# Two key tiles of the memory attention move from the tail into the latent attention

## The chip, the cores and the metric

The kernel runs on one core of a Trainium2 chip. The metric is the time on the device in microseconds (us), the median of several executions; lower is better.

## The reference

Two transformer blocks of different kind run one after the other, each two layers deep, on 512 tokens of width 1024 (float32). The change lies in the second block. Of one of its layers this matters here:

```
y_a, y_b, y_c = three mixers of other kinds          # 256 columns each
y_d = mla(...)          # "latent attention": 4 heads of 96, 512 x 512 scores
cat = rms_norm of [y_a, y_b, y_c, y_d], in four groups of 256 columns
x = x + cat @ w_out
hq = rms_norm(x, g_xq);  mn = rms_norm(mem, g_mem)   # mem: 256 rows of 1024
q = hq @ x_wq;  k, v = split(mn @ x_wkv)             # "memory attention"
o = attention(rms_norm(q), rms_norm(k), v);  x = x + o @ x_wo
x = x + (silu(a1) * a3) @ f_w2
```

The keys k of the memory attention need only the memory and the weights, nothing of x.

## The kernel before

**Weights.** Every weight matrix comes in tiles of 128 x 1024, which pass one stream (class `Weights`). SP loads a tile (L352) into one of two `raw` buffers (`RING`) as soon as the low part of the tile two places before it is made. ScalarE (ACT) makes its high part (L361, `split_high`), GpSimd (POOL) its low part (L370, `split_low`), into three buffers each (`PARTS`). TensorE (PE) multiplies a tile by activations that are split in the same way: three matmuls for each 128 rows (L384 to L386, `product`), 24 for a tile. The order of the tiles is fixed; the two key tiles have the numbers `base` and `base + 1`, the eight of w_out follow, then query and value tiles.

**Stages.** A stage is a block in which each engine has its own list of instructions; semaphores join them, and all engines meet at a barrier (L331) at its end. In a layer of the second block the mixers are followed by `second_attention` (the latent attention) and `second_tail` (norm of cat, w_out, memory attention, feed-forward part).

**The latent attention.** `attention_work` writes 16 units (4 heads by 4 blocks of 128 queries), n = 0 to 15. For each, PE multiplies the scores (L737), VectorE (DVE) takes the maximum (L835) and its negative (L838), ACT the exponentials (L799), DVE the reciprocal of their sum (L848, in the next step), POOL the scaled probabilities (L874), PE transposes them ("turn", L745), ACT copies the transposed block (L808), and after eight units PE multiplies by the values (L751, "values"). A turn comes four steps after its scores. PE goes in steps of two units: scores of n and n + 1, turns of n - 4 and n - 3, and at steps 12 and 20 the values. Each engine has side work between its steps. On DVE and ACT that is the preparation of the memory (`memory_prep`, class `Prep`): in steps 3 to 10 DVE makes high parts (L517), low parts (L527) and sums of squares (L534) of the eight chunks of the memory, in steps 2 to 9 ACT the squares (L523). ACT splits a weight tile in steps 10, 12 and 14, POOL behind units 12 and 14. POOL multiplies branch b (L2350) behind units 8 and 10. After its last copy (unit 15) ACT loads a table, does two SiLU, loads a table again and squares four tiles (L2319 to L2324), then copies the last values out (L817).

**The tail's start.** PE sums squares over the partitions for the four groups of cat (`group_sum`, L2424, four instructions each), and between them does the total of the memory (L539, L2434) and the two key tiles:

```
group_sum(0); group_sum(1); memory.total(...); columns
key_tile(0)
group_sum(2)
group_sum(3)
key_tile(1)
pe.wait_ge(sem("cat_log"), 4)
```

ACT makes Ln and Exp of each group's sum (L2525, L2527), then splits the tile `base + 3`, then makes the high parts of chunks 0 to 3 of cat (L2520). DVE multiplies the norm in (L2619) and makes the low parts (L2624). The first w_out matmul on PE waits for the low part of chunk 0, and each further chunk k of the first two w_out tiles for its own low part. The square of the keys (L2537), their sum over a head and the finished keys (L2650) come while PE is at the w_out tiles. The change and the prediction touch these places.

Of the kernel before, what the change touches and what calls it, by code (L numbers as in the profile page):

```python
# [18 lines left out]
ALU = mybir.AluOpType  # L19
ACT = mybir.ActivationFunctionType  # L20
# [3 lines left out]
P = 128  # L24
SEQ = 512
NT = SEQ // P
D = 1024
# [4 lines left out]
EPS = 1e-6  # L32
MEM = 256
# [552 lines left out]
def build(nc, x_in, w1, small1, const_in, p_in, w2, small2, masks_in, mem_in, pos_in, out):  # L586
    sem = Semaphores(nc)
# [9 lines left out]
    S = sb("slots", [P, SLOTS, SEQ])  # L597
# [7 lines left out]
    tmp = sb("tmp", [P, 10, SEQ])  # L605
# [17 lines left out]
    def cst(name):  # L623
        a, b = CONST.at[name]
        return const[:, a:b]
# [5 lines left out]
    def s2(name, i=0, n=1):  # L631
        a, _ = SECOND_SMALL.at[name]
        return small[:, a + i:a + i + n]
# [1664 lines left out]
    def second_attention(layer, weights, memory):  # L2298

        base = weights.used  # L2300

        def before(sp):
            sp.dma_start(S[:, MEM_RAW:MEM_RAW + 4, :].rearrange("p a (b n) -> p (a b) n", b=2), mem_in).then_inc(sem("load_mem"), 16)

        def first_act(act):
            for slot in (DEVIATION, B_R, B_R + 1):
                act.activation(S[:, slot, :], S[:, slot, :], ACT.Exp, scale=-0.5).then_inc(sem("late_rstd"), 1)

        def side_act(act, step):
            if step == 2:  # L2310
                act.wait_ge(sem("load_mem"), 16)
            if 2 <= step < 2 + KC:
                memory.square(act, step - 2)
            if step in (10, 12, 14):
                weights.split_high(act, base + step // 2 - 4)
            if step == 4 * NT + 3:
                for c in range(2):
                    act.wait_ge(sem("standard"), c + 1)
                    act.activation(S[:, Y + c, :], S[:, TAP_A + c, :], ACT.Silu, scale=s2("ln_g", c), bias=s2("ln_b", c)).then_inc(sem("branch_a"), 1)  # L2319
                act.preload_act_table_set(LOG_EXP)  # L2320
                act.wait_ge(sem("branch_a"), 2)
                act.wait_ge(sem("branch_b"), 2)
                for n in range(4):
                    act.activation(tmp[:, n, :], S[:, Y + n, :], ACT.Square).then_inc(sem("early_square"), 1)  # L2324

        def side_dve(dve, step, place):
            if place == "end" and step in (3, 4):
                a = S[:, TAP_A + step - 3, :]
                if step == 3:
                    dve.wait_ge(sem("late_rstd"), 3)  # L2330
                dve.tensor_tensor(a, a, S[:, DEVIATION, :], ALU.mult).then_inc(sem("standard"), 1)
            if place == "end" and step in (5, 6):
                c = step - 5
                y = S[:, Y + 2 + c, :]
                dve.scalar_tensor_tensor(y, y, s2("onorm", c), S[:, B_R + c, :], ALU.mult, ALU.mult).then_inc(sem("b_normed"), 1)
            if place == "scores" and step == 3:
                dve.wait_ge(sem("load_mem"), 16)
            if place == "scores" and 3 <= step < 3 + KC:
                memory.high_dve(dve, step - 3)
                if step >= 4:  # L2340
                    memory.add(dve, step - 3)
            if place == "end" and 3 <= step < 3 + KC:
                memory.low(dve, step - 3)

        def side_pool(pool, n):
            if n in (8, 10):
                c = (n - 8) // 2
                y = S[:, Y + 2 + c, :]
                pool.wait_ge(sem("b_normed"), c + 1)
                pool.tensor_tensor(y, y, S[:, G + c, :], ALU.mult).then_inc(sem("branch_b"), 1)  # L2350
            if n in (12, 14):
                weights.split_low(pool, base + n // 2 - 5)

        attention(weights, base + 3, attention_work(one(
            4, 1, 96 ** -0.5, lambda h, m, i: S[0:96, MQ + h, i * P:i * P + P], lambda h, m, L: S[0:96, MK + h, 0:L],
            lambda i: SEQ, None, lambda h, j: S[:, MV + j // 2, (j % 2) * 256 + 64 * h:(j % 2) * 256 + 64 * h + 64], 64,
            lambda h: S[64 * (h % 2):64 * (h % 2) + 64, Y + 6 + h // 2, :], NT, False,
            query_col=lambda h, i: col[:, QUERY_R + 4 * h + i:QUERY_R + 4 * h + i + 1]),
            side_act=side_act, side_dve=side_dve, side_pool=side_pool), before, first_act)

    def second_tail(layer, weights, memory, lead):

        base = weights.used
        out_at = base + 2
        q_at = out_at + KC
        o_at = q_at + 4
# [41 lines left out]
        with nc.Block() as block:  # L2408
# [10 lines left out]
            def _(pe):  # L2419
                def group_sum(g):  # L2420
                    if g >= 2:
                        pe.wait_ge(sem("cat_square"), 2 * g - 2)
                    for c in range(2):
                        mm = pe.matmul(banks[7 - g][:, :], cst("ones"), tmp[:, 2 * g + c, :], start=(c == 0), stop=(c == 1))  # L2424
                    mm.then_inc(sem("cat_summed"), 1)

                def key_tile(c):
                    dense(pe, weights, banks[2][:, c * MEM:c * MEM + MEM], memory.pairs)

                group_sum(0)  # L2430
                group_sum(1)
                memory.total(pe, banks[3][:, 0:MEM], cst("ones"), carried=True)
                for i in range(2):
                    mm = pe.matmul(banks[3][:, MEM + i:MEM + i + 1], memory.acc[:, i * P:i * P + P], cst("ones")[:, 0:1], start=True, stop=True)  # L2434
                mm.then_inc(sem("mem_columns"), 1)
                key_tile(0)
                group_sum(2)
                group_sum(3)
                key_tile(1)
                pe.wait_ge(sem("cat_log"), 4)  # L2440
                two = []
                for g in range(4):
# [36 lines left out]
                    mm.then_inc(sem("tile_done"), 1)  # L2479

                pe.wait_ge(sem("x_mixed"), KC)
                value_half(0)
                for c in range(2):
                    pe.wait_ge(sem("query_square"), c + 1)
# [29 lines left out]
            def _(act):  # L2514
# [7 lines left out]
                for g in range(4):  # L2522
                    act.wait_ge(sem("cat_summed"), g + 1)
                    r = tmp[:, 2 * g + 1, :]
                    act.activation(r, banks[7 - g][:, :], ACT.Ln, scale=1.0 / 256, bias=eps).then_inc(sem("cat_log"), 1)  # L2525
                    act.wait_ge(sem("cat_log"), g + 1)
                    act.activation(r, r, ACT.Exp, scale=-0.5).then_inc(sem("cat_rstd"), 1)  # L2527
                    if g == 1:
                        act.wait_ge(sem("mem_columns"), 1)
                        act.activation(col[:, MEM_R:MEM_R + 2], banks[3][:, MEM:MEM + 2], ACT.Ln, scale=1.0 / D, bias=eps).then_inc(sem("mem_column"), 1)  # L2530
                        act.wait_ge(sem("mem_column"), 1)
                        act.activation(col[:, MEM_R:MEM_R + 2], col[:, MEM_R:MEM_R + 2], ACT.Exp, scale=-0.5).then_inc(sem("mem_rstd"), 1)
                weights.split_high(act, base + 4)
                for n in range(4):
                    cat_high(n)
                act.wait_ge(sem("tile_done"), base + 2)
                act.activation(K_SQ, banks[2][:, :], ACT.Square).then_inc(sem("key_square"), 1)  # L2537
                weights.split_high(act, base + 5)
                for n in range(4, KC):
                    cat_high(n)  # L2540
# [73 lines left out]
            def _(dve):  # L2614
# [16 lines left out]
                normed(3)  # L2631
                dve.wait_ge(sem("mem_total"), 1)
                dve.wait_ge(sem("mem_columns"), 1)
                dve.tensor_scalar(E64_MEM, banks[3][:, 0:MEM], 64 * EPS / D, 64 * EPS * EPS, ALU.mult, ALU.add).then_inc(sem("mem_eps"), 1)
                cat_low(2)
                cat_low(3)
                for c in range(KC):
                    dve.wait_ge(sem("tile_done"), out_at + c + 1)
                    dve.tensor_tensor(S[:, X + c, :], S[:, X + c, :], banks[4 + c % 2][:, :], ALU.add).then_inc(sem("x_mixed"), 1)
                    hq.low(dve, c)  # L2640
                    if c >= 1:
                        hq.add(dve, c)
                    if c == 3:
                        dve.wait_ge(sem("key_sum"), 1)
                        dve.wait_ge(sem("mem_eps"), 1)
                        dve.tensor_tensor(K_R.rearrange("p (a n) -> p a n", a=2), banks[3][:, :].rearrange("p (a n) -> p a n", a=2),
                                          E64_MEM.unsqueeze(1).to_broadcast([P, 2, MEM]), ALU.add).then_inc(sem("key_biased"), 1)
                    if c == 5:
                        dve.wait_ge(sem("key_rstd"), 1)
                        dve.scalar_tensor_tensor(S[:, XK, :], banks[2][:, :], s2("x_kn"), K_R, ALU.mult, ALU.mult).then_inc(sem("key_ready"), 1)  # L2650
                dve.wait_ge(hq.sig("total"), 1)
                dve.tensor_scalar(E64, banks[6][:, :], 64 * EPS / D, 64 * EPS * EPS, ALU.mult, ALU.add).then_inc(sem("query_eps"), 1)
                dve.wait_ge(sem("query_eps"), 1)
# [94 lines left out]
```

## Time and profile before

| what | us |
|---|---|
| median of 3 executions | 3237.43 (3234.82 to 3238.01) |
| the profiled execution, its own time | 3235.97 |
| span of the profiled execution, first to last instruction | 3234.2 |
| latent attention, first of the two layers, from the trace | 1911.7 to 1961.7 |
| start of its tail, up to the first w_out matmul | 1961.7 to 1978.1 |
| latent attention, second layer | 2692.5 to 2743.2 |
| start of its tail, up to the first w_out matmul | 2743.2 to 2759.6 |

The mean granted clock of TensorE over the span is 0.987 of the full 2.4 GHz. Times in the trace count from the start of the span. In a row of a timeline, what stands in brackets is how long the engine sat idle before the instruction, and who ended that; PEq is the sequencer of TensorE, "issue" is a wait that the profile can't name. PE is the matmul, PEld the loading of its weights. "xN" joins N instructions in a row.

### The profile page before, as it was taken

How to read it: one execution, taken by the hardware profiler on the slowest of the kernel's cores; microseconds unless marked ns; L12 is line 12 of the kernel's file. 1: busy time of each engine (PE TensorE's matmuls, PEld its weight loads, DVE VectorE, ACT ScalarE, POOL GpSimd, SP SyncE). 2: the span in 40 equal slices, each digit the busy share in tenths (PEclk: the TensorE clock that was granted, in tenths of full speed). 3: DMA queues.
4: the chain of work that ended last, by engine and by line, in shares of the span. 5: the costliest groups of instructions: out<-in, count | busy, mean ns of one | idle time of the engine just before them, and what ended most of it. 6: DMA issues, size and time to landing. Idle time of an engine off the chain costs nothing. (4 is left out here: it accounts for less than half of the span.)

```text
span 3234.2 us, 38506 instructions
## 1 busy us (share of the span) xinstructions
PE 3076.4 (95%) x14372; PEld 2395.9 (74%) x14372; DVE 1624.8 (50%) x2472; ACT 1343.9 (42%) x2218; POOL 1589.8 (49%) x870
## 2 busy tenths in 40 slices
PE   8989999999999999999999988899999987989999
PEld 6766788888766678888887746688888763768887
DVE  3873357732477435774348754433224954443321
ACT  4446533333443654333342475532233267452221
POOL 5635655554663455555565343344445534344443
PEclk9999999999999999999999999999999998999999
DMA  4211233233221123333322102133332201223333
GB/s 134 66 59 46 85 101 96 97 111 98 89 70 60 46 75 102 98 98 108 106 97 79 47 14 65 59 104 92 98 109 93 72 27 33 72 72 98 98 98 104
DMA packets 73737, 265.05 MB, mean 82 GB/s; under 512 B 8656, under 2 KB 9168, under 8 KB 73168
## 3 DMA queue, kind: packets, MB, share of 16 engines
q1 hardware_dynamic: 73552, 262.59, 25.7%
q8 instruction: 115, 1.88, 0.2%
q14 instruction: 70, 0.57, 0.1%
HBM read 260.46 MB, written 2.10 MB: 81 GB/s over the span
## 5 line engine op out<-in xcount | busy, mean ns | idle before, releaser
L370 POOL TENSOR_TENSOR low<-raw,high 128x1024 fp32r<-128x1024 f32 x482 | 1178.7, 2447 | 1157.0 <-ACT high L361 1120.8
L385 PE MATMUL bank<-slot_r,low 128*128 128x512 f32 (+1 forms) x3652 | 1427.5, 391 | 0.0
L386 PE MATMUL bank<-slot_r,high 128*128 128x512 f32 (+1 forms) x3652 | 1425.4, 390 | 0.0
L384 PE MATMUL bank<-slot_r,high 128*128 128x512 f32 (+1 forms) x3332 | 1326.3, 398 | 45.4 <-POOL low L370 14.9
L361 ACT ACTIVATE high<-raw 128x1024 fp32r<-128x1024 f32 x482 | 508.2, 1056 | 908.4 <-PE bank L386 838.5
L386 PEld LDWEIGHTS bank<-slot_r,high 128*128 128x128 f32 x3652 | 689.2, 189 | 148.3
L385 PEld LDWEIGHTS bank<-slot_r,low 128*128 128x128 f32 x3652 | 689.5, 189 | 146.0 <-issue 6.7
L384 PEld LDWEIGHTS bank<-slot_r,high 128*128 128x128 f32 x3332 | 629.4, 189 | 216.8 <-issue 50.3
L1618 DVE SCALAR_TENSOR_TENSOR tmp<-padded,small,tmp 128x512 f32<-128x512 f32 x176 | 210.0, 1252 | 0.0
L874 POOL TENSOR_SCALAR tmp<-tmp,stat 128x512 f32<-128x512 f32 (+3 forms) x128 | 80.3, 628 | 148.3 <-DVE stat L848 123.0
L2107 DVE SCALAR_TENSOR_TENSOR slots<-padded,small,slots 128x512 f32<-128x512 f32 x128 | 140.4, 1154 | 0.0
L1609 DVE TENSOR_TENSOR padded<-bank,rs 128x512 f32<-128x512 f32 x88 | 60.4, 687 | 138.6 <-PE bank L386 128.9
L2677 DVE TENSOR_TENSOR tmp<-bank,rs 128x512 f32<-128x512 f32 x44 | 30.4, 692 | 191.9 <-PE bank L386 186.7
L737 PE MATMUL bank<-slots 64*128 64x256 f32 (+4 forms) x384 | 97.3, 509 | 22.2 <-PEq L331 19.3
L527 DVE SCALAR_TENSOR_TENSOR slot_r<-slots,small,slot_r 128x512 fp32r<-128x512 f32 (+1 forms) x80 | 92.8, 1160 | 44.1 <-ACT slot_r L514 43.8
L808 ACT ACTIVATE PT<-bank 128x256 f32<-128x256 f32 (+3 forms) x160 | 72.0, 454 | 102.4 <-PE bank L751 58.6
L2589 ACT ACTIVATE tmp<-tmp 128x512 f32<-128x512 f32 x44 | 28.0, 636 | 203.1 <-DVE tmp L2677 203.1
L2687 DVE TENSOR_TENSOR tmp<-bank,rs 128x512 f32<-128x512 f32 x16 | 11.1, 691 | 193.9 <-PE bank L386 193.9
L745 PE MATMUL bank<-const,tmp 128*128 128x128 f32 x432 | 72.7, 291 | 36.7 <-ACT PT L808 27.9
L1361 DVE TENSOR_TENSOR slot_r<-tmp,slot_r 128x512 fp32r<-128x512 f32 x48 | 75.6, 1575 | 59.4 <-ACT slot_r L2582 59.4
L745 PEld LDWEIGHTS bank<-const,tmp 128*128 128x128 f32 x432 | 51.7, 146 | 67.8 <-issue 38.9
L384 PE MATMUL bank<-pt_r,high 128*128 128x512 f32 x256 | 101.6, 397 | 0.0
(310 smaller groups left out, 3165.8 us busy)
## 6 DMA issues: line engine op xcount, KB each, us to landing
raw<-w SPq DMA_DIRECT2D x482, 512.0 KB, 3.6
slots<-x_in SPq DMA_DIRECT2D x4, 512.0 KB, 6.6
slots<-mem_in SPq DMA_DIRECT2D x2, 1024.0 KB, 4.8
out<-slots SPq DMA_DIRECT2D x8, 256.0 KB, 5.1
const<-const_in SPq DMA_DIRECT2D x1, 1073.5 KB, 10.7
padded<-p_in SPq DMA_DIRECT2D x2, 512.0 KB, 5.6
tmp<-masks_in SPq DMA_DIRECT2D x1, 512.0 KB, 11.5
small<-small SPq DMA_DIRECT2D x2, 231.5 KB, 2.9
```

Of the source, the lines that this page charges most:

```text
L361: act.activation(self.high[:, t % PARTS, :], self.raw[:, t % RING, :], ACT.Copy).then_inc(self.sem("tile_high"), 1)
L370: pool.tensor_tensor(self.low[:, t % PARTS, :], self.raw[:, t % RING, :], self.high[:, t % PARTS, :].bitcast(F32), ALU.subtract).then_inc( ...
L384: pe.matmul(acc, lhs[0], rhs[1], start=first, stop=False)
L385: pe.matmul(acc, lhs[1], rhs[0], start=False, stop=False)
L386: return pe.matmul(acc, lhs[0], rhs[0], start=False, stop=last)
L527: dve.scalar_tensor_tensor(self.pairs[c][1], self.xs[c], self.gain[c], self.pairs[c][0].bitcast(F32), ALU.mult, ALU.subtract).then_inc(sel ...
L737: pe.matmul(banks[s % 4][:, 0:width(n)], a["q"](h, m, i), a["k"](h, m, width(n)), start=True, stop=True).then_inc(sem("scored"), 1)
L745: mm = pe.transpose(banks[4 + n % 2][:, j * P:j * P + P], prob(n)[:, j * P:j * P + P], cst("ident"))
L874: pool.tensor_scalar(prob(n), tmp[:, E + s % 4, 0:width(n)], st(3, s), 1.0, ALU.mult, ALU.mult).then_inc(sem("prob_ready"), 1)
L1361: dve.tensor_tensor(parts[g][1], tmp[:, 6 + g % 2, :], parts[g][0].bitcast(F32), ALU.subtract).then_inc(sem("hidden_low"), 1)
L1618: dve.scalar_tensor_tensor(o, padded_t[:, s % 4, 15 - tap:15 - tap + SEQ], s1("conv_w", (2 - tap) * 2 * FC + ch), o, ALU.mult, ALU.add).th ...
L2107: ins = dve.scalar_tensor_tensor(o, src, s2(w, 2 * j + c), o, ALU.mult, ALU.add)
```

## The change

The two key tiles are multiplied in the latent attention, in PE's steps 14 and 16, behind the turns (turns 10 and 11, and 12 and 13), into bank 7, which that attention does not use. So that the tiles are there, ACT splits in steps 6, 8 and 14 instead of 10, 12 and 14, and POOL behind units 7 and 9 instead of 12 and 14; the third tile's low part is made at the start of the tail, as before. In the tail the key tiles fall away, the group sums and the memory's total use other banks (6 to 3, and 2), and one wait for the finished keys stands ahead of the value tiles, which write bank 7. No instruction is added or dropped but waits.

```diff
@@ second_attention
-            if step in (10, 12, 14):
-                weights.split_high(act, base + step // 2 - 4)
+            if step in (6, 8, 14):
+                weights.split_high(act, base + {6: 1, 8: 2, 14: 3}[step])
...
-            if n in (12, 14):
-                weights.split_low(pool, base + n // 2 - 5)
+            if n in (7, 9):
+                weights.split_low(pool, base + (n - 5) // 2)
+
+        def side_pe(pe, step, place):
+            if place == "turns" and step in (14, 16):
+                c = (step - 14) // 2
+                dense(pe, weights, banks[7][:, c * MEM:c * MEM + MEM], memory.pairs, norm=memory)
...
@@ second_tail
-        base = weights.used
+        base = weights.used - 2
...
-                        mm = pe.matmul(banks[7 - g][:, :], cst("ones"), tmp[:, 2 * g + c, :], start=(c == 0), stop=(c == 1))
+                        mm = pe.matmul(banks[6 - g][:, :], cst("ones"), tmp[:, 2 * g + c, :], start=(c == 0), stop=(c == 1))
...
-                def key_tile(c):
-                    dense(pe, weights, banks[2][:, c * MEM:c * MEM + MEM], memory.pairs)
...
-                memory.total(pe, banks[3][:, 0:MEM], cst("ones"), carried=True)
+                memory.total(pe, banks[2][:, 0:MEM], cst("ones"), carried=True)
...
-                key_tile(0)
                 group_sum(2)
                 group_sum(3)
-                key_tile(1)
                 pe.wait_ge(sem("cat_log"), 4)
...
                 pe.wait_ge(sem("x_mixed"), KC)
+                pe.wait_ge(sem("key_ready"), 1)
                 value_half(0)
...
-                act.wait_ge(sem("tile_done"), base + 2)
-                act.activation(K_SQ, banks[2][:, :], ACT.Square).then_inc(sem("key_square"), 1)
+                act.activation(K_SQ, banks[7][:, :], ACT.Square).then_inc(sem("key_square"), 1)
...
-                        dve.scalar_tensor_tensor(S[:, XK, :], banks[2][:, :], s2("x_kn"), K_R, ALU.mult, ALU.mult).then_inc(sem("key_ready"), 1)
+                        dve.scalar_tensor_tensor(S[:, XK, :], banks[7][:, :], s2("x_kn"), K_R, ALU.mult, ALU.mult).then_inc(sem("key_ready"), 1)
```

## Rows read from the trace of the kernel before

**Rows 1.** The page: busy time of each engine.

```profile
PE 3076.4 (95%) x14372; PEld 2395.9 (74%) x14372; DVE 1624.8 (50%) x2472; ACT 1343.9 (42%) x2218; POOL 1589.8 (49%) x870
```

**Rows 2.** Stages: PE, PEld, DVE, ACT, POOL busy, clock, DMA, GB/s.

```profile
1911.70:1961.70 50.00, 36.35 (x128) 17.36 (x128) 25.81 (x75) 37.08 (x74) 21.60 (x20) 0.86 0.10 32
...
1978.00:1992.00 14.00, 13.93 (x48) 11.01 (x48) 9.87 (x13) 3.04 (x5) 2.83 (x1) 0.78 0.27 75
...
2759.50:2772.90 13.40, 12.77 (x48) 9.86 (x48) 10.03 (x13) 3.04 (x6) 2.83 (x1) 0.89 0.24 78
```

**Rows 3.** Chain that ended last, second tail: start, us, what.

```profile
2750.70 3.45 PE bank L2424 x8
...
2754.17 0.70 ACT tmp L2525
...
2755.43 1.05 ACT high L361
...
2757.03 1.61 DVE slot_r L2624
```

**Rows 4.** Timeline of PE, first tail: start, us, idle before.

```profile
1961.78 3.67 PE L2424 MATMUL bank<-tmp,const 128*128 128x512 f32 x8 [3.04 <-PEq L331]
...
1966.08 0.37 PE L384 MATMUL bank<-slot_r,high 128*128 128x256 f32 x1
...
1969.05 3.60 PE L2424 MATMUL bank<-tmp,const 128*128 128x512 f32 x8
...
1972.08 0.68 PE L384 MATMUL bank<-slot_r,high 128*128 128x256 f32 x1
...
1978.07 0.77 PE L384 MATMUL bank<-slot_r,high 128*128 128x512 f32 x1 [2.57 <-issue]
```

**Rows 5.** Timelines of ACT, DVE and POOL where DVE and POOL overlap.

```profile
1931.81 0.78 ACT L799 ACTIVATE tmp<-bank,stat,col 128x512 f32<-128x512 f32 x1 [0.24 <-DVE stat L838]
...
1931.69 0.34 DVE L517 TENSOR_SCALAR slot_r<-slots,small 128x256 fp32r<-128x256 f32 x1
...
1933.59 1.18 DVE L517 TENSOR_SCALAR slot_r<-slots,small 128x256 fp32r<-128x256 f32 x1
...
1937.43 0.67 DVE L835 TENSOR_REDUCE stat<-bank 128x1 f32<-128x512 f32 x1
...
1975.54 2.43 DVE L2624 TENSOR_TENSOR slot_r<-tmp,slot_r 128x512 fp32r<-128x512 f32 x1 [7.25 <-ACT slot_r L2520]
...
1930.63 0.85 POOL L874 TENSOR_SCALAR tmp<-tmp,stat 128x512 f32<-128x512 f32 x1 [1.05 <-DVE stat L848]
...
1933.35 1.27 POOL L2350 TENSOR_TENSOR slots<-slots 128x512 f32<-128x512 f32 x1
...
1937.23 1.27 POOL L2350 TENSOR_TENSOR slots<-slots 128x512 f32<-128x512 f32 x1
...
1975.07 2.36 POOL L370 TENSOR_TENSOR low<-raw,high 128x1024 fp32r<-128x1024 f32 x1 [10.88 <-ACT high L361]
```

**Rows 6.** Timelines of PE and ACT, end of the first latent attention.

```profile
1945.67 0.63 PE L745 MATMUL bank<-const,tmp 128*128 128x128 f32 x4 [1.16 <-ACT PT L808]
...
1949.87 2.78 PE L745 MATMUL bank<-const,tmp 128*128 128x128 f32 x12 [1.57 <-ACT PT L808]
...
1953.34 5.40 PE L751 MATMUL bank<-PT,slots 128*64 128x512 f32 x16 [0.69 <-ACT PT L808]
...
1942.26 0.60 ACT L808 ACTIVATE PT<-bank 128x512 f32<-128x512 f32 x1 [3.70 <-PE bank L751]
...
1943.23 1.05 ACT L361 ACTIVATE high<-raw 128x1024 fp32r<-128x1024 f32 x1
...
1952.68 0.60 ACT L808 ACTIVATE PT<-bank 128x512 f32<-128x512 f32 x1 [0.42 <-PE bank L745]
```

**Rows 7.** Stages: PE, PEld, DVE, ACT, POOL busy, clock, DMA, GB/s.

```profile
1911.70:1919.60 7.90, 7.82 (x21) 3.83 (x22) 5.08 (x15) 5.65 (x13) 2.38 (x3) 0.78 0.39 133
...
2692.50:2700.30 7.80, 7.74 (x13) 3.27 (x14) 4.20 (x13) 4.82 (x11) 1.51 (x3) 0.67 0.37 134
```

More of the change, by code:

```diff
@@ L2358, in second_attention @@
             query_col=lambda h, i: col[:, QUERY_R + 4 * h + i:QUERY_R + 4 * h + i + 1]),
-            side_act=side_act, side_dve=side_dve, side_pool=side_pool), before, first_act)
+            side_pe=side_pe, side_act=side_act, side_dve=side_dve, side_pool=side_pool), before, first_act)
     def second_tail(layer, weights, memory, lead):
-        base = weights.used
+        base = weights.used - 2
         out_at = base + 2
@@ L2423, in group_sum @@
                     for c in range(2):
-                        mm = pe.matmul(banks[7 - g][:, :], cst("ones"), tmp[:, 2 * g + c, :], start=(c == 0), stop=(c == 1))
+                        mm = pe.matmul(banks[6 - g][:, :], cst("ones"), tmp[:, 2 * g + c, :], start=(c == 0), stop=(c == 1))
                     mm.then_inc(sem("cat_summed"), 1)
-                def key_tile(c):
-                    dense(pe, weights, banks[2][:, c * MEM:c * MEM + MEM], memory.pairs)
                 group_sum(0)
                 group_sum(1)
-                memory.total(pe, banks[3][:, 0:MEM], cst("ones"), carried=True)
+                memory.total(pe, banks[2][:, 0:MEM], cst("ones"), carried=True)
                 for i in range(2):
-                    mm = pe.matmul(banks[3][:, MEM + i:MEM + i + 1], memory.acc[:, i * P:i * P + P], cst("ones")[:, 0:1], start=True, stop=True)
+                    mm = pe.matmul(banks[2][:, MEM + i:MEM + i + 1], memory.acc[:, i * P:i * P + P], cst("ones")[:, 0:1], start=True, stop=True)
                 mm.then_inc(sem("mem_columns"), 1)
-                key_tile(0)
                 group_sum(2)
                 group_sum(3)
-                key_tile(1)
                 pe.wait_ge(sem("cat_log"), 4)
@@ L2524, in _ @@
                     r = tmp[:, 2 * g + 1, :]
-                    act.activation(r, banks[7 - g][:, :], ACT.Ln, scale=1.0 / 256, bias=eps).then_inc(sem("cat_log"), 1)
+                    act.activation(r, banks[6 - g][:, :], ACT.Ln, scale=1.0 / 256, bias=eps).then_inc(sem("cat_log"), 1)
                     act.wait_ge(sem("cat_log"), g + 1)
@@ L2529, in _ @@
                         act.wait_ge(sem("mem_columns"), 1)
-                        act.activation(col[:, MEM_R:MEM_R + 2], banks[3][:, MEM:MEM + 2], ACT.Ln, scale=1.0 / D, bias=eps).then_inc(sem("mem_column"), 1)
+                        act.activation(col[:, MEM_R:MEM_R + 2], banks[2][:, MEM:MEM + 2], ACT.Ln, scale=1.0 / D, bias=eps).then_inc(sem("mem_column"), 1)
                         act.wait_ge(sem("mem_column"), 1)
@@ L2633, in _ @@
                 dve.wait_ge(sem("mem_columns"), 1)
-                dve.tensor_scalar(E64_MEM, banks[3][:, 0:MEM], 64 * EPS / D, 64 * EPS * EPS, ALU.mult, ALU.add).then_inc(sem("mem_eps"), 1)
+                dve.tensor_scalar(E64_MEM, banks[2][:, 0:MEM], 64 * EPS / D, 64 * EPS * EPS, ALU.mult, ALU.add).then_inc(sem("mem_eps"), 1)
                 cat_low(2)
```

## Prediction

> **What bounds the kernel now.** I read the page first. TensorE is busy for 95% of the span [rows 1], so over the whole kernel PE sets the pace, and time can be won or lost only where it idles or is slow. The table of stages shows that the latent attention is such a place: in 50.0 us PE works 36.4, ACT 37.1, DVE 25.8, POOL 21.6, and the granted clock is 0.86 on average [rows 2]. No engine is full there; a chain of short instructions across four engines sets the end. The idea of the change is that PE has room in it.
>
> The next view is the chain that ended last, at the start of the tail. It goes through PE's last group sums, ACT's Ln and Exp, ACT's split of a w_out tile (L361), ACT's high part of cat and DVE's low part of it, to the first w_out matmul [rows 3]. On PE's own timeline the first key tile stands ahead of the last two group sums, from 1966.08 to 1969.05, and so on that chain. The second one starts at 1972.08, behind the last sum, and ends 2.57 us before PE's next matmul, at 1975.50 [rows 4]. It is hidden: PE waits anyway for the low part of chunk 0, which DVE ends at 1977.97 [rows 5].
>
> **What the tail gives back.** With both key tiles gone, group sums 2 and 3 begin at 1966.1 instead of 1969.05. Ln, Exp, ACT's split, the high parts, POOL's split of that tile and DVE's low parts follow with the same distances, since none of them waits for anything else: the weight tile was asked for at the start of the stage, and the square of the keys, which stands in ACT's queue behind chunk 3, had its tile at 1975.5 and needs no wait now either. The gain is the first key tile, 1969.05 - 1966.08 = 3.0 us. The second (1975.50 - 1972.08 = 3.4 us) gives nothing; PE idles 2.57 + 3.4 = 6.0 us there instead. So 3.0 of 6.4 us per layer come back. The bank changes cost nothing, and the new wait for the keys stands where all eight chunks of x are mixed, while DVE finishes the keys at the sixth; what hides it is PE's work on the last w_out tiles, and if that cover were gone it would cost DVE's one pass.
>
> **What the attention pays for the matmuls.** PE's turns 10 and 11 end at 1946.3, and the next is late in the stage; turns 13 to 15 start at 1949.87 and the last values at 1953.34, as soon as ACT has copied unit 15 (1952.68 plus 0.60) [rows 6]. From that copy on ACT runs through its table loads, SiLU and squares without a pause to the end, so the copy of unit 15 sets the end of the stage. Now the new order. ACT's split in step 12 (1943.23, 1.05 us) falls away; it stood behind the wait for the values and so on the chain, and all that follows comes about 0.95 earlier (the next instruction starts a little before the end). Turn 11 ends at 1945.67 - 0.95 + 0.63 = 1945.35. Key tile 0 lasts 3.4 behind transposes, as key tile 1 did behind the float32 sums: 1948.75. Turn 12 to 1949.4, turn 13 to 1950.0, key tile 1 to 1953.4, turns 14 and 15 (0.5 each) to 1954.4, where ACT begins its last copy instead of at 1952.68. That is +1.7; with 3.1 for a key tile (24 matmuls at the distance of the first one's, 2.97 in all [rows 4]) it is +1.2. I take +1.5. Below that lies 0, if PE had room after all, and above it +1.5 plus 3.0 for each key tile that meets half clock, which stood at 0.5 in part of this stage (the 5.40 us of the last values [rows 6]).
>
> **What the attention pays for the earlier splits.** ACT's splits (1.05 us) in steps 6 and 8 meet small gaps: ACT waits 0.24 us for DVE at the exponential of unit 9 [rows 5], so the second makes it up to 0.8 late, but DVE asks for that result only a step later. POOL's are another matter. Before, they lay behind units 12 and 14, where DVE stood still; the first now starts when POOL has scaled unit 7, at 1930.63 + 0.85 = 1931.48, in the middle of DVE's busiest stretch, and DVE's maximum and negative are what ACT waits for there. The trace has such a collision: DVE's high part L517, 0.34 us alone, took 1.18 when POOL multiplied branch b from 1933.35 to 1934.62, and ended 0.15 after POOL; the low part L2624 took 2.43 beside a split and ended 0.54 after it [rows 5]. POOL's split lasts 2.36 us, so to 1933.84. DVE's L517 of that step starts at 1931.69 and would end at 1933.99 instead of 1932.03: +2.0 us for DVE, and with it for maximum, exponential, copy, turns and values, up to ACT's copy behind the values (a wait of 3.70 us [rows 6]) and on to the end. The second split, behind unit 9, falls on maxima, negatives and reciprocals, and a maximum is not stretched by POOL: 0.67 us at 1937.43 beside POOL's 1.27 at 1937.23 [rows 5]. It delays POOL's units 10 to 12, whose turns come only in PE's steps 14 and 16, behind the last wait for the values: nothing. Bounds: 0 if DVE gets through, 2.0 as worked out, and 4.4 if both splits hold DVE up. I take 2.0.
>
> The Trainium skill (SBUF — State Buffer, "Who interferes with whom") calls the port pair that DVE and GpSimd share an exclusive lock, held for a whole instruction, and says that a reduction never takes it. By that rule the first split costs 2.0 us a layer and the second nothing; if every DVE instruction could be held up, the sum below would be 2 x 2.4 = 4.8 us higher. The rule speaks against this change, and the trace agrees with it (1.18 against 0.34, and 0.67 unchanged).
>
> **What the clock pays.** The granted clock follows PE's work. In the first stretch after the barrier that opens the attention it was 0.78 of full over 7.9 us in one layer and 0.67 over 7.8 us in the other [rows 7]; at 1.2 instead of 2.4 GHz that is a loss of (1 - 0.78) x 7.9 = 1.7 and 2.6 us of PE time. Ahead of the group sums PE idled 3.04 us and kept the full clock [rows 4]. Now the last values run behind dense key tiles, probably at full clock and so shorter than 5.40, and PE waits longer for the barrier. The sums are on the chain, so a drop costs there between 0 and 2.6 us; I take half of 1.7, 0.8. At the first w_out tiles the clock drops already: 0.78 over 14.0 us in the first layer, 0.89 over 13.4 in the second [rows 2], so at half for 6.2 and 2.9 us. That is 3.1 and 1.5 us of PE time lost. A longer idle could give the second layer the first's case, or the other way round: 1.6, less the 0.6 that PE idled in the second's (12.77 busy of 13.4) behind DVE's low parts. So 0 in the sum, 1.0 in the bounds.
>
> **Sum.** Per layer -3.0 + 1.5 + 2.0 + 0.8 = +1.3 us, twice +2.6. Against the profiled execution's own time (3235.97, span 3234.2) that is 3238.6; the median of the runs lies 1.5 higher, so 3237.4 + 2.6 = 3240.0. About 0.2%, 6.5 us, is what a measurement of this kernel can tell from no change.
>
> **The rivals.**
> *The splits hide.* POOL's first split finds DVE outside the instructions that collide, and costs 0; then twice (-3.0 + 1.5), 3234.4. For it: only three of DVE's instructions a step collide. Against it: L517 follows the split's start within 0.2 us.
> *The attention swallows everything.* Matmuls and splits fit into its idle time, as its 73% of PE would suggest; then 2 x -3.0 gives 3231.4, just short of a measurable gain. Against it: both tiles stand ahead of turns that ACT's last copies wait for.
> *All the key tiles' time comes back*, 2 x -(3.0 + 3.4), 3224.6. It needs the w_out tiles to start when PE is ready, and DVE's low part forbids that.
> *The clock falls at the group sums* (the other side): the longer idle before the tail lets it drop for about as long as behind the attention's first barrier, in both layers. Then per layer -3.0 + 1.5 + 2.0 + 2.6 + 1.0 = +4.1, 3245.6. It decides the sign from 2.8 us of clock a layer. For it: the same engine dropped twice after a barrier; against it, it did not after 3.04 us ahead of these very sums.
>
> **How the numbers follow.** My forecast holds with a chance of 0.60, hidden splits 0.12, everything swallowed 0.10 (a third of it beyond -6.5 us), all time back 0.01, the clock 0.17 (two thirds beyond +6.5 us). That makes faster 0.04, same 0.84, slower 0.12. The range reaches from between the second and first rival, 3233, to just past the clock's case, 3246; the forecast's own is 3237 to 3243.
>
> **What the profile after should show.** Key tiles in the first attention near 1947 and 1952, 3.1 to 3.4 us each; one L517 of some 2.3 us per layer beside a POOL split, and none for the second; the attention 3.5 us longer (53.5 us); the stretch from the tail's first group sum to the first w_out matmul 13.3 us instead of 16.3, with one idle of about 6 us in it; nothing else moved. I am wrong if L517 keeps 0.34, if a key tile takes 5 us or more, if the group sums run slow, or if the tail's start shrinks by more than 3 us.

## The result, and the profile after

The changed kernel takes 3245.5 us (median of 10 runs, 3242.1 to 3246.7) against 3237.0 (10 runs, 3232.4 to 3238.6) of the kernel before on the same chip: a ratio of 1.0028, 95% interval 1.0018 to 1.0038. It is slower by 8.5 us, and the interval leaves out 1. The prediction had 3240.0, 0.84 for no change that can be measured and 0.12 for a slower kernel; the measured time lies just inside its range, which ended at 3246.

The profiled execution has a span of 3243.5 us instead of 3234.2. Two stages of each layer hold most of the difference. I measure them on PE's timeline, from the first scores (L737) to the first group sum, from there to the first w_out matmul, and from there to the sum over the squared keys (L2459).

| us | attention | tail's start | w_out to keys' sum | sum |
|---|---|---|---|---|
| before, layer 1 | 50.00 | 16.29 | 25.16 | 91.45 |
| after, layer 1 | 54.13 | 15.62 | 25.07 | 94.82 |
| before, layer 2 | 50.72 | 16.28 | 24.37 | 91.37 |
| after, layer 2 | 55.09 | 15.70 | 25.08 | 95.87 |

Both layers together are 7.9 us longer. The attention grew by 4.1 and 4.4 where 3.5 was forecast, and the tail's start shrank by 0.6 and 0.7 instead of 3.0. Here is DVE's and POOL's timeline of the changed kernel, the answer to [rows 5]:

```profile
1930.97 0.35 DVE L517 TENSOR_SCALAR slot_r<-slots,small 128x256 fp32r<-128x256 f32 x1
...
1932.88 2.27 DVE L517 TENSOR_SCALAR slot_r<-slots,small 128x256 fp32r<-128x256 f32 x1
...
1936.70 1.17 DVE L517 TENSOR_SCALAR slot_r<-slots,small 128x256 fp32r<-128x256 f32 x1
...
1940.52 0.67 DVE L835 TENSOR_REDUCE stat<-bank 128x1 f32<-128x512 f32 x1
...
1932.64 2.35 POOL L370 TENSOR_TENSOR low<-raw,high 128x1024 fp32r<-128x1024 f32 x1
...
1939.19 2.34 POOL L370 TENSOR_TENSOR low<-raw,high 128x1024 fp32r<-128x1024 f32 x1
```

L517 starts 0.24 us into POOL's first split and ends 0.16 after it: 2.27 instead of 0.34, 1.9 us more where 2.0 were forecast. A maximum beside the second split keeps 0.67. This part went as written down.

PE's and ACT's timelines show what was not. Turn 9 and the first values of the kernel before come first, since its rows above begin later:

```profile
1937.95 0.63 PE L745 MATMUL bank<-const,tmp 128*128 128x128 f32 x4 [1.37 <-ACT PT L808]
1938.50 3.65 PE L751 MATMUL bank<-PT,slots 128*64 128x512 f32 x16
```

The changed kernel, from turn 8 to the last values, with ACT's copy behind the first values (beside [rows 6]); the last three rows are the tail, beside [rows 4]:

```profile
1938.32 0.63 PE L745 MATMUL bank<-const,tmp 128*128 128x128 f32 x4 [0.88 <-ACT PT L808]
1941.04 1.09 PE L745 MATMUL bank<-const,tmp 128*128 128x128 f32 x4 [2.10 <-ACT PT L808]
1942.06 4.74 PE L751 MATMUL bank<-PT,slots 128*64 128x512 f32 x16
...
1949.74 0.36 PE L384 MATMUL bank<-slot_r,high 128*128 128x256 f32 x1
...
1952.70 0.60 PE L745 MATMUL bank<-const,tmp 128*128 128x128 f32 x4
...
1956.88 1.03 PE L745 MATMUL bank<-const,tmp 128*128 128x128 f32 x8
1958.65 3.65 PE L751 MATMUL bank<-PT,slots 128*64 128x512 f32 x16 [0.74 <-ACT PT L808]
...
1946.90 0.60 ACT L808 ACTIVATE PT<-bank 128x512 f32<-128x512 f32 x1 [5.25 <-PE bank L751]
...
1967.09 5.90 PE L2429 MATMUL bank<-tmp,const 128*128 128x512 f32 x8 [4.79 <-PEq L331]
...
1973.62 3.68 PE L2429 MATMUL bank<-tmp,const 128*128 128x512 f32 x8
...
1982.71 0.77 PE L384 MATMUL bank<-slot_r,high 128*128 128x512 f32 x1 [5.41 <-issue]
```

The four transposes of turn 9 take 1.09 us at 1941.04 instead of 0.63, and the first values right behind them 4.74 instead of 3.65; ACT waits for them 5.25 us instead of 3.70. The eight instructions of the first group sums take 5.90 instead of 3.67, behind an idle time of 4.79 instead of 3.04. The stages show why (behind the busy times of PE, PEld, DVE, ACT and POOL stands the granted clock):

```profile
1942.00:1946.80 4.80, 4.80 (x18) 1.41 (x17) 0.00 (x0) 0.00 (x0) 2.76 (x4) 0.76 0.00 0
...
1958.60:1962.30 3.70, 3.65 (x16) 1.06 (x16) 0.00 (x0) 3.65 (x5) 0.00 (x0) 1.00 0.00 0
1962.30:1967.10 4.80, 0.01 (x3) 0.04 (x1) 0.00 (x0) 3.73 (x8) 0.00 (x0) 0.76 0.00 0
1967.10:1973.00 5.90, 5.90 (x9) 2.58 (x10) 0.74 (x2) 3.48 (x6) 2.36 (x1) 0.62 0.66 178
1973.00:1977.30 4.30, 4.30 (x14) 1.99 (x13) 2.09 (x4) 2.99 (x6) 0.00 (x0) 1.00 0.00 0
```

Ahead of the group sums the clock falls to its lower level while PE idles, 0.76 over the 4.8 us, and stays there for most of the sums. Ahead of the first values it was still 0.96 over the 2.1 us of idle time, then 0.50 over turn 9, 0.54 over the first 2.5 us of the values and 1.00 over the rest. A key tile, on the other hand, takes only 2.96 us (1949.74 to 1952.70).

### The profile page after: what moved, and what is told of

The parts are those of the page before. It is cut to its first block and busy times, and to the rows that moved or that the text cites. A ratio compares the mean times of both kernels' runs of the same rounds, so it can differ in the third digit from the quotient of the medians.

```text
span 3243.5 us, 38510 instructions
## 1 busy us (share of the span) xinstructions
PE 3081.1 (95%) x14372; PEld 2398.3 (74%) x14372; DVE 1628.4 (50%) x2472; ACT 1340.8 (41%) x2218; POOL 1588.8 (49%) x870
## 5 line engine op out<-in xcount | busy, mean ns | idle before, releaser
L737 PE MATMUL bank<-slots 64*128 64x256 f32 (+4 forms) x384 | 97.8, 510 | 22.1 <-PEq L331 19.3
L799 ACT ACTIVATE tmp<-tmp,stat 128x128 f32<-128x128 f32 (+3 forms) x128 | 71.0, 556 | 66.3 <-DVE stat L832 65.6
```

Of the source, the lines that this page charges most:

```text
L737: pe.matmul(banks[s % 4][:, 0:width(n)], a["q"](h, m, i), a["k"](h, m, width(n)), start=True, stop=True).then_inc(sem("scored"), 1)
```

## The experiments

The theory after this reading, for layer 1: -2.9 for the key tile that leaves the chain, +0.7 for the matmuls in the attention, +1.9 for DVE behind POOL's split, +1.5 for the clock at the first values, +2.2 for the clock at the group sums; 3.4 in all. The rivals: that the matmuls are the main loss, or that the slow stretches would be there whatever one did. The lengths of the stages of all runs, both layers, stand in a table below the last experiment; each ratio is against runs of the kernel before on the same chip. The median of that kernel was 3237.0 beside the changed kernel and 3237.1, 3236.5 or 3235.7 beside the experiments, so two kernels compare better by their ratios than by their times. A stage's length comes from one profiled execution, whose time lies up to 2.6 us beside the median.

**Late low parts.** The changed kernel with

```diff
-            if n in (7, 9):
-                weights.split_low(pool, base + (n - 5) // 2)
+            if n in (9, 11):
+                weights.split_low(pool, base + (n - 7) // 2)
```

> The changed kernel, but POOL makes the low parts behind units 9 and 11 of the latent attention instead of 7 and 9, where DVE has finished the memory's chunks. Theory (each layer pays 1.9 us because POOL's first split holds up DVE's L517, and through the wait that this causes PE loses its full clock at the first values, another 1.5 us): L517 beside a split back from 2.27 to 0.34 us, values at 3.65 instead of 4.74, the attention 3 to 3.5 us shorter per layer, in all 6 to 7 us faster than the changed kernel, within 2 us of the kernel before. Rival (the collision is real but other engines would have waited anyway; the loss is the key tiles' matmuls and the clock in the tail): less than 2 us in all.

Measured: 3238.8 us, ratio 1.0004 (0.9995 to 1.0013). No L517 over 1.18, the values at 3.65, the attention 50.67 and 51.52: 3.5 us shorter than after the change, in both layers. Two numbers and nothing else take 6.7 us away, as forecast (6 to 7). The group sums stay slow (6.04 and 6.06).

**Splits alone.** The kernel before with ACT's splits in steps 6, 8 and 14 and POOL's behind units 7 and 9; the key tiles stay in the tail.

> The kernel before with only the splits moved (ACT in steps 6, 8, 14; POOL behind units 7 and 9); the key tiles stay in the tail. Theory: this alone costs 1.9 us of DVE a layer, and 1 to 1.5 us more where the clock falls at the first values, less 0.95 for ACT's split that leaves step 12: the attention 2 to 2.5 us longer per layer, the tail as before, 4 to 5 us slower than the kernel before. Rival (the splits are free, the matmuls are the loss): within 1 us of the kernel before.

Measured: 3241.6 us, 1.0019 (1.0010 to 1.0028), 4.5 us slower without one matmul moved. The attention is 2.3 and 1.6 longer, L517 takes 2.26, the values 5.26. The tail did not stay as before, which the forecast had missed: its start took 17.97 and 17.98 instead of 16.3, because the first group sums ran at 5.37, here behind an idle time of only 2.35 us.

```profile
1955.80:1962.10 6.30, 6.23 (x16) 1.63 (x16) 0.00 (x0) 6.26 (x9) 0.00 (x0) 0.59 0.00 0
1962.10:1964.40 2.30, 0.02 (x1) 0.05 (x1) 0.00 (x0) 1.21 (x3) 0.00 (x0) 1.00 0.00 0
1964.40:1969.80 5.40, 5.40 (x10) 2.36 (x11) 0.35 (x1) 3.48 (x7) 2.35 (x1) 0.68 0.57 192
```

These three are the last values, the idle time and the first sums. From the first scores to the keys' sum both layers of this kernel add up to 6.6 us more than before, in a profiled execution 2.2 us above the median; with the tail's loss in it, the median met the forecast of 4 to 5 partly by luck. The length of the gap ahead of the sums does not decide by itself; the clock was low in the values before it, back at 1.00 in the gap, and low again in the sums.

**Matmuls alone.** The changed kernel with the splits where they were (ACT in steps 10, 12, 14; POOL behind units 12 and 14).

> The changed kernel with the splits where they were (ACT in steps 10, 12, 14; POOL behind units 12 and 14); the key tiles stay in the attention. Theory: DVE's L517 at 0.34 and the values at 3.65; but the second key tile must wait for its low part until about 50.4 of the old time scale, so it ends near 53.5 and ACT's last copy comes 1.5 to 2 us late; the group sums still meet half clock (+2.2 us), the tail gives 3.0: the attention +1.5 to +2, the tail's start -0.7, in all 2 to 3 us slower than the kernel before. Rival (matmuls are the main loss): attention +3 or more per layer.

Measured: 3238.8 us, 1.0008 (0.9999 to 1.0017). The attention is 1.8 and 2.0 longer, the second key tile waiting for its low part; the tail's start is 15.08. For the attention that is what the theory gave, and not the 3 or more of the rival. The group sums took 5.37, 1.7 us over full clock where 2.2 was forecast, and the kernel is 1.7 us slower instead of 2 to 3; its interval does not tell it from the kernel before.

**Filler ahead of the tail.** The changed kernel with matmuls whose result nobody reads (filler), behind the last values

```diff
+            if place == "end" and step == 4 * NT + 4:
+                for _ in range(4):
+                    pe.matmul(banks[5][:, :], cst("ones"), S[:, MEM_RAW, :], start=True, stop=True)
```

> The changed kernel with four more float32 matmuls (into bank 5, read by nobody) on PE behind the last values of the latent attention, where PE waits for the barrier. Theory (PE's idle time of 4.8 us before the tail lets the clock fall, and the eight instructions of the first group sums take 5.9 instead of 3.7): idle about 1.3 us, the group sums back to 3.7, 2.2 us less per layer, 4 to 5 us faster than the changed kernel. Rival (the clock falls after the attention whatever PE does last, or the added work makes the barrier late): the group sums stay at 5.9 and the time is the same or longer.

Measured: 3241.2 us, 1.0014 (1.0006 to 1.0023), 4 us less than the changed kernel, as forecast. Work that nobody reads makes the kernel faster. Its PE in the first tail:

```profile
1968.06 3.67 PE L2434 MATMUL bank<-tmp,const 128*128 128x512 f32 x8 [1.15 <-PEq L331]
...
1981.45 0.77 PE L384 MATMUL bank<-slot_r,high 128*128 128x512 f32 x1 [5.41 <-issue]
```

The sums are back at 3.67 and the tail's start is 13.39, in the other layer 13.40: 2.9 us shorter than before the change. That is the gain that the prediction took from the trace (3.0), freed of the clock.

**Filler ahead of the first values.** The changed kernel with two float32 matmuls into bank 7 behind the scores of step 12, where PE waits.

> The changed kernel with two more float32 matmuls (into bank 7, overwritten by the key tiles) on PE behind the scores of step 12, where PE waits for ACT before turns 8 and 9. DVE is still held up by POOL's split. Theory (the lock costs 1.9 us by itself, and the second loss at the first values, 1.1 us in them and 0.4 in the turn ahead, is the clock, which falls because PE idles longer): values back to 3.7, attention up to 1.5 us shorter per layer, in all 2 to 3 us faster than the changed kernel, with L517 still at 2.27. Rival (the values are slow for another reason that the split brings): values stay at 4.7.

Measured: 3239.7 us, 1.0012 (1.0003 to 1.0021). That is some 5 us less than the changed kernel: 4.6 with each held against the kernel before that ran beside it, 5.2 by the stages, more than the 2 to 3 of the forecast. Turn 9 and the values:

```profile
1939.81 0.63 PE L745 MATMUL bank<-const,tmp 128*128 128x128 f32 x4 [1.45 <-ACT PT L808]
1940.37 3.65 PE L751 MATMUL bank<-PT,slots 128*64 128x512 f32 x16
```

L517 is still 2.26, the values are 3.65, the attention 52.58 and 52.59 instead of 54.13 and 55.09. So the stall of DVE alone leaves 1.9 of the loss (52.58 against 50.67 with late low parts), and the clock at the values made 1.55 more in layer 1 (2.5 in layer 2, where the attention's first scores also ran faster, 7.08 against 7.93). The tail's group sums stayed slow, 5.14 us behind 4.79 of idle time, and cost more in layer 2 (a start of 16.42) than in layer 1 (14.86).

**Both splits in DVE's busy stretch.** POOL's splits behind units 7 and 8.

> The changed kernel with POOL's splits behind units 7 and 8 instead of 7 and 9, so that the second one falls into DVE's work on the memory as well. Theory (the cost is DVE waiting for POOL's whole instruction, not the splits as such): one more instruction of DVE with two inputs in SBUF (the sum of squares L534 or the high part L517) takes about 2.5 instead of 0.4 us, attention about 2 us longer per layer than in the changed kernel, in all 4 us slower than it. Rival (only the first split matters): the same as the changed kernel.

Measured: 3247.5 us, 1.0037 (1.0023 to 1.0050). Over the changed kernel that is 2.0 us by the medians, 3.3 with each held against the kernel before that ran beside it and 4.0 by the stages, where 4 was forecast. The attention is 57.06 and 56.90, 2.9 and 1.8 longer than after the change. DVE and POOL of this kernel:

```profile
1929.42 0.42 DVE L534 TENSOR_TENSOR slots<-slots 128x256 f32<-128x256 f32 x1
...
1935.98 2.57 DVE L534 TENSOR_TENSOR slots<-slots 128x256 f32<-128x256 f32 x1
...
1935.87 2.39 POOL L370 TENSOR_TENSOR low<-raw,high 128x1024 fp32r<-128x1024 f32 x1
```

The sum of squares, 0.42 us alone, takes 2.57: a second collision adds a second stall, and again the values get slower (5.52). What costs is where the split falls, not that it is early. The Trainium skill (SBUF — State Buffer, "Who interferes with whom") says that `tensor_tensor` "has no 2-port mode, but with both inputs in SBUF it contends with GpSimd's reads"; this run agrees, with 2.57 us against 0.42.

**Late low parts and filler.** Both remedies together.

> POOL's splits behind units 9 and 11, both key tiles in steps 14 and 16, and four idle float32 matmuls behind the last values. Theory: the two costs are independent and add up: attention 50.7 and 51.5, group sums 3.7, tail's start 13.4; 184.0 - 4.7 = 179.3 us for both layers from the first scores to the keys' sum, where the kernel before takes 182.8: 3.5 us faster. Rival (one cost hides the other): the gain over late splits alone is under 2 us.

Measured: 3233.3 us, 0.9990 (0.9982 to 0.9999). The stages make 178.05 us, 4.8 less than before where 3.5 was forecast, and 5.95 less than with late low parts alone, where the rival had under 2: neither cost hides the other.

**One tile.** Only the first key tile moves (step 14), the second stays in the tail behind the group sums, the splits stay.

```diff
             if place == "turns" and step == 14:
                 dense(pe, weights, banks[7][:, 0:MEM], memory.pairs, norm=memory)
...
                 group_sum(2)
                 group_sum(3)
+                dense(pe, weights, banks[7][:, MEM:2 * MEM], memory.pairs)
```

> Only the first key tile moves to the attention (behind the turns of step 14); the second stays in the tail, behind the group sums, where PE waits; the splits stay where they were. Theory: nothing collides with DVE; the attention grows by at most 0.5 us, the tail's start gives 3.0 us back, but the last values run at full clock, PE idles 4.8 us before the tail and the group sums take 1.7 to 2.3 us more: 0.5 to 1 us faster per layer, in all 1 to 2 us faster than the kernel before. Rival (the idle time matters less than what ran before it; the second tile was not hidden in the tail): group sums at 3.7 and 5 to 6 us faster, or the w_out tiles late by 3 us and no gain.

Measured: 3233.1 us, 0.9991 (0.9982 to 1.0000). The w_out tiles start on time behind the second tile, and the group sums are slow (5.09 and 6.73), as the theory had it. The kernel is 3.3 us faster than before, where 1 to 2 was forecast. But the attention did not grow: 49.23 in both layers, 0.8 and 1.5 less than before with 3 us more matmuls in it. PE's timeline there:

```profile
1951.02 0.60 PE L745 MATMUL bank<-const,tmp 128*128 128x128 f32 x4
1951.87 1.16 PE L745 MATMUL bank<-const,tmp 128*128 128x128 f32 x8 [0.25 <-ACT PT L808]
1953.27 0.63 PE L745 MATMUL bank<-const,tmp 128*128 128x128 f32 x4 [0.25 <-ACT PT L808]
1954.59 3.65 PE L751 MATMUL bank<-PT,slots 128*64 128x512 f32 x16 [0.69 <-ACT PT L808]
```

Two things do it. Before, PE idled 1.37 and 1.57 us ahead of turns 12 and 13; the key tile fills that time, and turn 13 starts 38.1 us behind the first scores in both kernels. And behind it the clock is 1.00, so turns 13 to 15 take 1.79 us, where they took 2.78 at a clock of 0.54 [rows 6]; the last values start 0.8 us earlier. Of the 1.5 us in layer 2 the other 0.8 is not the edit's: the first scores of that stage took 7.09 us instead of 7.88. And layer 1 loses 1.6 us behind the tail's start (26.03 to the keys' sum, 24.38 in layer 2): there PE began w_out at full clock, ran into a wait of 1.83 us for DVE's low part and went on at 0.62 over the next 4 us.

**One tile and filler.** The same with four float32 matmuls behind the last values.

> One key tile in the attention, the other in the tail, splits where they were, and four idle float32 matmuls behind the last values. Theory: as with one tile, and the group sums at full clock: attention up to 50.5, tail's start 13.4, 5 us faster than the kernel before. Rival: no better than one tile without the added matmuls.

Measured: 3225.5 us (5 runs), 0.9968 (0.9955 to 0.9980). Attention 49.23, tail's start 13.41. It is 11 us faster than before, 8.7 by the stages, where 5 was forecast.

**Second tile at the end of the attention.** The changed kernel with POOL's splits behind units 9 and 11, and

```diff
-            if place == "turns" and step in (14, 16):
-                c = (step - 14) // 2
+            if (step, place) in ((14, "turns"), (4 * NT + 4, "end")):
+                c = 0 if step == 14 else 1
```

> The changed kernel with POOL's splits behind units 9 and 11, and the second key tile behind the last values of the attention instead of behind turns 12 and 13. It then fills PE's idle time before the barrier. Theory: last copy about 0.7 us earlier than with the tile in step 16, attention 49.5 to 50, idle before the tail about 1.9 instead of 4.8 and with it group sums at 3.7, the tail's start 13.3: 3 us faster per layer, in all 6 us faster than the kernel before (3231). Rival (the clock falls at the tail whatever fills the gap, or PE's end makes the barrier late): within 2 us of the kernel before.

Measured: 3224.3 us (5 runs), 0.9965 (0.9953 to 0.9978), 12 us less than before, where 6 was forecast (9.8 by the stages). It does the work of the change and no filler: the second tile is itself what keeps PE busy. PE's timeline of its first layer:

```profile
1951.54 3.65 PE L751 MATMUL bank<-PT,slots 128*64 128x512 f32 x16 [0.69 <-ACT PT L810]
...
1955.12 0.38 PE L384 MATMUL bank<-slot_r,high 128*128 128x256 f32 x1
...
1964.28 3.68 PE L2431 MATMUL bank<-tmp,const 128*128 128x512 f32 x8
```

The stages of this kernel from the last values through the group sums:

```profile
1951.50:1958.20 6.70, 6.66 (x40) 3.98 (x40) 0.00 (x0) 6.66 (x9) 0.00 (x0) 1.00 0.01 2
1958.20:1960.00 1.80, 0.07 (x2) 0.05 (x1) 0.00 (x0) 0.74 (x3) 0.00 (x0) 1.00 0.00 0
1960.00:1968.00 8.00, 7.96 (x22) 3.73 (x22) 2.83 (x4) 6.45 (x12) 2.36 (x1) 1.00 0.41 131
```

The gap is 1.8 us instead of 4.8, and the clock is 1.00 in all three. The attention (48.28 in layer 1) is 2.4 us shorter than with both tiles ahead of the turns (50.67, late low parts), and 0.95 shorter than with one tile (49.23): that is ACT's split, gone from step 12, the 0.95 of the prediction.

**Filler ahead of w_out.** That kernel with five float32 matmuls into bank 1 behind the group sums.

> The kernel with the second key tile behind the last values (POOL's splits behind units 9 and 11), and five more float32 matmuls into bank 1 behind the tail's group sums, where PE idles 5.4 us before the first w_out tile. Theory: the clock is kept, the first w_out matmuls run at full clock, but DVE's low parts limit the first two tiles anyway: up to 0.7 us less per layer, about 1 us faster than that kernel (3223). Rival (the half clock at the first w_out tiles is a main loss): 2.5 to 3 us per layer.

Measured: 3224.0 us (5 runs), 0.9967 (0.9954 to 0.9979): the same as without filler, and not the 1 us that was forecast. The stage from the first w_out matmul, without and with filler:

```profile
1973.30:1983.20 9.90, 9.83 (x34) 7.81 (x35) 9.34 (x12) 3.05 (x5) 2.82 (x1) 0.79 0.36 106
```

```profile
1973.10:1983.00 9.90, 8.03 (x34) 6.36 (x35) 9.34 (x12) 3.00 (x5) 2.86 (x1) 1.00 0.34 106
```

The clock is 1.00 instead of 0.79, PE is busy for 8.03 us instead of 9.83, and the stage ends no earlier (24.39 against 24.41 to the keys' sum). DVE, at 9.34 in both, sets the end; with filler PE now waits for its low part:

```profile
1980.69 0.50 PE L384 MATMUL bank<-slot_r,high 128*128 128x512 f32 x1 [1.82 <-DVE slot_r L2628]
```

All runs, stages in us, layer 1 / layer 2:

| kernel | attention | tail's start | both layers, to the keys' sum | median, ratio |
|---|---|---|---|---|
| before | 50.00 / 50.72 | 16.29 / 16.28 | 182.8 | |
| changed | 54.13 / 55.09 | 15.62 / 15.70 | 190.7 | 3245.5, 1.0028 |
| late low parts | 50.67 / 51.52 | 15.76 / 15.78 | 184.0 | 3238.8, 1.0004 |
| splits alone | 52.33 / 52.30 | 17.97 / 17.98 | 189.5 | 3241.6, 1.0019 |
| matmuls alone | 51.77 / 52.68 | 15.08 / 15.08 | 184.6 | 3238.8, 1.0008 |
| filler before the tail | 54.16 / 54.13 | 13.39 / 13.40 | 184.1 | 3241.2, 1.0014 |
| filler before the values | 52.58 / 52.59 | 14.86 / 16.42 | 185.5 | 3239.7, 1.0012 |
| both splits collide | 57.06 / 56.90 | 16.02 / 15.93 | 194.7 | 3247.5, 1.0037 |
| late and filler | 51.46 / 50.66 | 13.39 / 13.39 | 178.1 | 3233.3, 0.9990 |
| one tile | 49.23 / 49.23 | 14.83 / 16.47 | 180.2 | 3233.1, 0.9991 |
| one tile and filler | 49.23 / 49.23 | 13.41 / 13.41 | 174.1 | 3225.5, 0.9968 |
| second tile at the end | 48.28 / 49.14 | 13.39 / 13.40 | 173.0 | 3224.3, 0.9965 |
| that, filler before w_out | 48.26 / 49.09 | 13.41 / 13.41 | 173.0 | 3224.0, 0.9967 |

A difference of 0.8 us in the attention need not be the edit's: its first twelve score instructions took about 7.1 us in some stages and 7.9 in others (7.87 and 7.08 in the two layers of late and filler), with nothing changed ahead of them in that stage. That is also why layer 2 grew less than layer 1 in the splits alone (7.08 against 7.88 before) and where both splits collide (7.09 against 7.93 in the changed kernel).

## Why the prediction was wrong

It named the parts and missed the sum: +1.3 us per layer forecast, +3.4 and +4.5 measured. By its own steps:

- *The tail gives back 3.0.* Right as to the chain: 2.9 us with the clock held up (filler before the tail, 13.39 against 16.29). The second key tile gave nothing, as forecast; PE idled 5.41 there instead of 2.57, and not the 6.0 of the text: the 3.4 us of the second tile are counted from the start of its row, 1972.08, while the row of the sums ahead of it lasts to 1972.65.
- *The matmuls in the attention, +1.5.* Measured +0.7 (late low parts: 50.67 against 50.00). The path was right and a size was off: a key tile takes 2.96 behind transposes, not 3.4, and with 2.96 twice in place of 3.4 the text's own chain gives +0.8. The turns behind a key tile stood in that chain at full-clock lengths (0.6, and 0.5 each) and took them. For one tile alone the text's bound of 0 was nearer: it fits into PE's waits, and the attention came out 0.8 us shorter.
- *POOL's first split, +2.0; the second, nothing.* Measured +1.9, a maximum beside the second unstretched (0.67), and the doubled collision gave a second stall of the same kind.
- *The clock, +0.8.* This is the step that failed. The term was put at half of 1.7 us and at the group sums alone. It measured 2.2 to 2.3 there in both layers. And there was a second place, which the sum did not have: the first values. I passed the 2.0 us of DVE's delay down the chain as a bare shift. But PE waits during a shift. Its idle time grew from 0 to 0.88 before turn 8 and from 1.37 to 2.10 before turn 9, the clock fell, and the turn and the sixteen matmuls of the values, all on the chain, cost 1.5 us more. Filling the wait before turn 8 gave it back with DVE still held up.
- *The w_out tiles, 0 in the sum.* -0.1 and +0.7 us; within the bounds. The 0.7 is the case that the text named: over the 14 us from the first w_out matmul the second layer's clock was 0.90 before and 0.79 after, as in the first layer (0.78 and 0.79). Where it was 0.85, in the kernel with the second tile at the end, the last filler shows that a higher one gives nothing more.

The rival that put the clock's fall at the group sums gave 3245.6, next to the measured 3245.5, but partly by luck: it had the right mechanism at one of its two places, and in layer 1 its 0.4 too much there, 1.0 for w_out tiles and 0.8 too much for the matmuls outweighed the 1.5 at the values that it lacked. Its chance of 0.17 was too low. The reason given against it, that the clock had held behind an idle time of 3.04 us, compared a gap of 3.0 with one of 4.8, though the text itself had worked out that the gap would grow.

What remains open is the rule by which the clock falls. A gap of 4.8 us ahead of the sums brought it down in every run, gaps of 1.2 to 1.8 in none, one of 3.0 in neither layer of the kernel before; but in the splits alone one of 2.3 to 2.4 did, behind values partly at half clock, and in the kernel before the last turns ran at 0.54 with no gap over 1.57 us ahead of them. Where exactly it falls also differs between layers of one run (5.09 and 6.73 us for the same sums with one tile). And PE's wait of 1.8 us at a w_out tile was followed by a clock of 0.62 over 4 us with one tile, but by 1.00 in the splits alone (1.84 us) and with filler ahead of w_out (1.82). The medians differ a little more than the stages: 8.5 us against 7.9 for the change, 12 against 9.8 for the kernel with the second tile at the end. The start of the first latent attention lies between 1911.2 and 1914.0 us in the runs, ahead of anything that was changed, so a part of such differences is not the edit's.

## What to carry to other kernels

A stall on a chain is not a shift: ask what TensorE does meanwhile, since a wait in front of dense or float32 work can cost its clock as well, here almost as much again as the stall. When work moves out of a stage, look at which gaps it leaves and which it could fill: the second key tile cost 2.4 us in front of the last turns, nothing at the end of the attention, and there it saved another 2.4 us at the sums behind the barrier. And here a long GpSimd instruction cost nothing where VectorE took maxima from PSUM or stood still, and its whole length beside VectorE's passes from SBUF to SBUF (L517, L534); two numbers in a list were worth 6.7 us.

## What was not expected of the hardware

- Matmuls whose result nobody reads made the kernel faster: four in each layer (3.7 us of PE's idle time) gave 4 us in all, and with them the eight instructions behind went from 5.90 to 3.67 us.
- A stage with 3 us more of matmuls was 0.8 us shorter (one tile, 49.23 against 50.00): they filled waits of PE, and the short transposes behind them ran at full clock.
- Full clock without effect: 1.00 instead of 0.79 over 9.9 us changed the stage's end by 0.02 us, with 9.34 us of VectorE's work in it either way.
